# Position bias added by VectorE from a 128-fold stored table, and second-block attention groups first

## What is computed

```python
# layer 0: 12 heads, banded, with a bias by distance; q and k are normed per head
bias = rel_bias[:, jnp.clip(rel, -REL_CLIP, REL_CLIP) + REL_CLIP]
s = einsum('bqhd,bkhd->bhqk', qc, kc) * scale + bias
s = jnp.where(valid, s, NEG_INF);  p = softmax(s);  o = p @ v
# layer 1: 6 pairs of heads, chunk mask, difference of two softmaxes, norm of each output
a = p[:, :, 0] - lam * p[:, :, 1];  o = rmsnorm(a @ v, b_subln) * (1.0 - lambda_init)
# both layers: 4 more heads attend to a memory, with no bias
# layer 2: 8 heads of 128, causal, with a T5 bias by distance
```

## Time and profile before

| | us |
|---|---|
| median of 3 runs | 2204.18 |
| lowest, highest | 2199.34, 2204.64 |
| the profiled execution's own time | 2210.05 |
| its span, first to last instruction | 2208.3 |

### The profile page before, as it was taken

How to read it: one execution, slowest core, us unless ns; L and a number is a source line. 1 busy time by engine, 2 the same in 40 slices (tenths; PEclk the granted TensorE clock), 3 DMA queues, 4 the chain that set the end, 5 groups by cost and what they waited for, 6 DMA issues and landing times.

```text
span 2208.3 us, 27753 instructions
## 1 busy us (share of the span) xinstructions
PE 2040.2 (92%) x11973; PEld 1392.1 (63%) x11973; DVE 837.6 (38%) x973; ACT 693.9 (31%) x917; POOL 35.1 (2%) x27
## 2 busy tenths in 40 slices
PE   7999999999999997899999999989888888989886
PEld 6998777899899876799977644433333333333332
DVE  5555644555555577555543521111111111111112
ACT  5444564544644455443434211111101000110010
POOL 6000000000000000000000000000000000000000
PEclk9999999999999998999999899999999999999998
DMA  8554606555455541355463699999999999999995
GB/s 278 193 191 152 210 11 209 160 190 184 150 193 190 171 153 58 115 191 183 141 210 115 267 403 428 427 428 428 427 428 428 427 428 428 427 428 427 427 428 215
DMA packets 164820, 604.21 MB, mean 274 GB/s; under 512 B 9204, under 2 KB 102336, under 8 KB 140052
## 3 DMA queue, kind: packets, MB, share of 16 engines
q1 hardware_dynamic: 164724, 602.82, 70.9%
HBM read 601.70 MB, written 1.09 MB: 273 GB/s over the span
## 4 chain that ended last, share of the span: by engine, by line
PE 61%; DMA 28%; ACT 5%; DVE 4%; issue 1%; SPq 1%; DVEq 0%; ACTq 0%
PE ps L1432 14%; PE ps L1434 14%; PE ps L1433 14%; DMA sb_raw<-in_moe_w_gate_up 10%; PE ps L1791 8%; DMA sb_w_free<-in_moe_w_gate_up 8%; DMA sb_nat_more<-in_moe_w_gate_up 6%; PE ps L1801 4%; DMA sb_raw<-in_moe_w_down 3%; PE ps L1606 1%; ACT sb_w_hi L589 1%; ACT sb_prob L704 1%; PE ps L1808 1%; PE ps L1774 1%; PE ps L1566 1%
## 5 line engine op out<-in xcount | busy, mean ns | idle before, releaser
L893 DVE TENSOR_TENSOR sb_w_lo<-sb_raw,sb_w_hi 128x2048 fp32r<-128x2048 f32 x180 | 415.7, 2312 | 369.3 <-ACT sb_w_hi L589 369.0
L589 ACT ACTIVATE sb_w_hi<-sb_raw 128x2048 fp32r<-128x2048 f32 x180 | 343.9, 1914 | 295.0 <-PE ps L1434 283.3
L1432 PE MATMUL ps<-sb_xT_hi,sb_w_hi 128*128 128x256 f32 x1408 | 397.3, 282 | 7.2 <-DVE sb_xT_lo L914 7.2
L1433 PE MATMUL ps<-sb_xT_lo,sb_w_hi 128*128 128x256 f32 x1408 | 396.2, 281 | 0.0
L1434 PE MATMUL ps<-sb_xT_hi,sb_w_lo 128*128 128x256 f32 x1408 | 396.1, 281 | 0.0
L1432 PEld LDWEIGHTS ps<-sb_xT_hi,sb_w_hi 128*128 128x128 f32 x1408 | 265.9, 189 | 9.8 <-issue 4.5
L1433 PEld LDWEIGHTS ps<-sb_xT_lo,sb_w_hi 128*128 128x128 f32 x1408 | 266.0, 189 | 1.6
L1434 PEld LDWEIGHTS ps<-sb_xT_hi,sb_w_lo 128*128 128x128 f32 x1408 | 266.0, 189 | 0.0
L1791 PE MATMUL ps<-sb_raw,sb_xs 128*64 128x512 f32 x784 | 177.5, 595 | 23.7 <-DMA sb_raw<-in_moe_w_gate_up 23.3
L1791 PE MATMUL ps<-sb_w_free,sb_xs 128*64 128x512 f32 x752 | 172.1, 602 | 27.0 <-DMA sb_w_free<-in_moe_w_gate_up 26.4
L1432 PE MATMUL ps<-sb_w_hi,sb_xT_hi 128*128 128x512 f32 x384 | 155.1, 404 | 9.2 <-DVE sb_xT_lo L914 4.7
(11 more groups left out here) (245 smaller groups left out, 2334.2 us busy)
## 6 DMA issues: line engine op xcount, KB each, us to landing
sb_raw<-in_moe_w_gate_up SPq DMA_DIRECT2D x49, 2048.0 KB, 35.4
sb_w_free<-in_moe_w_gate_up SPq DMA_DIRECT2D x47, 2048.0 KB, 35.3
sb_w_free<-in_moe_w_down SPq DMA_DIRECT2D x25, 2048.0 KB, 35.4
sb_raw<-in_moe_w_down SPq DMA_DIRECT2D x23, 2048.0 KB, 34.0
sb_raw<-in_ffn_w_gate SPq DMA_DIRECT2D x44, 1024.0 KB, 5.4
sb_raw<-in_ffn_w_up SPq DMA_DIRECT2D x44, 1024.0 KB, 5.3
sb_raw<-in_ffn_w_down SPq DMA_DIRECT2D x44, 1024.0 KB, 4.9
sb_late_raw<-in_moe_w_gate_up SPq DMA_DIRECT2D x16, 2048.0 KB, 35.4
```

Source lines behind the costliest of these rows:

```text
L589: sc.activation(w_hi[:, c % CUT, :], raw[:, c % RAW, :], ACT.Copy).then_inc(hi_made, 1)
L893: ve.tensor_tensor(w_lo[:, c % CUT, :], raw[:, c % RAW, :], w_hi[:, c % CUT, :].bitcast(F32), ALU.subtract).then_inc(lo_made, 1)
L1432: pe.matmul(o, l_hi, r_hi, start=start, stop=False)
L1433: pe.matmul(o, l_hi, r_lo, start=False, stop=False)
```

## The change

- `ext` in DRAM becomes 24 blocks of 128 rows of 512. `store_rows` writes each head's row 128 times (a source that repeats, 256 KB a head). `load_strips` reads at a pitch of 511, from element 127 on, so that partition p gets the window that begins at 127 - p: the strips are no longer reversed.
- The `flip` products of layers 0 and 2 are gone. `lead` adds strip and scores on VectorE (PSUM and SBUF in, `prob` in SBUF out), then takes the maximum from `prob`; `exps` reads `prob` in these groups. The waits for the strips go from TensorE to VectorE. Layer 1's mask stays a product.
- In all three attentions the groups of own heads of block 1 (256 keys) now come before those of block 0. Memory groups keep their order. Block 1's rows are turned first. In layer 1 the turn of block 1 comes after outputs(7), `sub_norm(1)` after outputs(6), `sub_norm(0)` after outputs(7), and both square roots after ScalarE's last copy.

```diff
+EXT_ROW = P * 512
-        ext = nc.dram_tensor("ext", (3, 12, 512), F32)
+        ext = nc.dram_tensor("ext", (2 * 12, EXT_ROW), F32)
-            order = [(b, h0) for b in range(TB) for h0 in (0, 4, 8)]
+            order = [(b, h0) for b in (1, 0) for h0 in (0, 4, 8)]
             if kind == "rel":
-                order = [(b, h0) for b in range(TB) for h0 in (0, 4)] + [(b, 8) for b in range(TB)]
+                order = [(b, h0) for b in (1, 0) for h0 in (0, 4)] + [(b, 8) for b in (1, 0)]
             if kind == "moba":
-                for b in range(TB):
+                for b in (1, 0):
...
                 sp.wait_ge(ext_copied, n + 1)
-                sp.dma_start(ext[n, 0:heads, :], row_by_distance(heads)).then_inc(ext_stored, 16)
+                dst = bass.AP(ext, n * 12 * EXT_ROW, [[EXT_ROW, heads], [512, P], [1, 512]])
+                src = row_by_distance(heads).unsqueeze(1).to_broadcast([heads, P, 512])
+                sp.dma_start(dst, src).then_inc(ext_stored, 16)
                 sp.wait_ge(ext_stored, 16 * (n + 1))
...
-                    src = bass.AP(ext, (n * 12 + h0 + h) * 512, [[1, P], [1, REL_W]])
+                    src = bass.AP(ext, (n * 12 + h0 + h) * EXT_ROW + P - 1, [[511, P], [1, REL_W]])
...
                     for h in range(4):
-                        src = ps[:, 2 * p + h % 2, (h // 2) * S:(h // 2) * S + g["nk"] * P]
+                        if g["bias"] and not g["diff"]:
+                            src = prob[:, p, h, 0:g["nk"] * P]
+                        else:
+                            src = ps[:, 2 * p + h % 2, (h // 2) * S:(h // 2) * S + g["nk"] * P]
...
+                        for c in range(2):
+                            ve.tensor_tensor(prob[:, p, 2 * c:2 * c + 2, 0:nk], s[:, c, :, 0:nk], rows,
+                                             ALU.add).then_inc(biased, 1)
+                        for c in range(2):
+                            ve.wait_ge(biased, biased_no[0] - 1 + c)
+                            ins = ve.tensor_reduce(soft[:, p, 2 * c:2 * c + 2], prob[:, p, 2 * c:2 * c + 2, 0:nk], AX.X,
+                                                   ALU.max, negate=True)
...
-                        if groups[n]["diff"] and n >= 5 and n != 6:
-                            sub_norm(int(n == 7))
+                        if groups[n]["diff"] and n >= 6:
+                            sub_norm(7 - n)
...
                         for h in pair:
-                            if g["bias"]:
-                                h0, _ = g["bias"]
+                            if g["diff"]:
                                 m0 = P if g["b"] == 0 else 0
-                                if kind == "diff":
-                                    ins = pe.matmul(at(h), flip_bf[:], chunk_mask[:, m0:m0 + nk], start=False, stop=True)
-                                else:
-                                    row = strip[:, h0 + h, m0:m0 + nk] if h0 < 8 else strip_b[:, h, m0:m0 + nk]
-                                    ins = pe.matmul(at(h), flip[:], row, start=False, stop=True)
+                                ins = pe.matmul(at(h), flip_bf[:], chunk_mask[:, m0:m0 + nk], start=False, stop=True)
...
                         if n == len(groups) - 1:
                             pe.wait_ge(prob_made, u0 + len(groups))
-                            first_block()
+                            if not g_last_diff:
+                                first_block()
                         outputs(n)
                         if n == 0:
                             scores(2)
+                    if g_last_diff:
+                        first_block()
```

More of the change, by code:

```diff
@@ L797, in _ @@
                     sub_root(1)
+                    sub_root(0)
                 turn(t_of(i, T_O))
@@ L1062, in lead @@
                         ve.wait_ge(probT_turned, u - 1)
-                    for c in range(2):
-                        ins = ve.tensor_reduce(soft[:, p, 2 * c:2 * c + 2], s[:, c, :, 0:g["nk"] * P], AX.X, ALU.max, negate=True)
+                    nk = g["nk"] * P
+                    if g["bias"] and not g["diff"]:
+                        if u0 == u_moba:
+                            ve.wait_ge(strip_loaded, 16 * 20)
+                        else:
+                            ve.wait_ge(strip_ready, g["bias"][0] // 8 + 1)
+                        m0 = P if g["b"] == 0 else 0
+                        for c in range(2):
+                            h0 = g["bias"][0] + 2 * c
+                            rows = strip[:, h0:h0 + 2, m0:m0 + nk] if h0 < 8 else strip_b[:, h0 - 8:h0 - 6, m0:m0 + nk]
+                            ve.tensor_tensor(prob[:, p, 2 * c:2 * c + 2, 0:nk], s[:, c, :, 0:nk], rows,
+                                             ALU.add).then_inc(biased, 1)
+                            biased_no[0] += 1
+                        for c in range(2):
+                            ve.wait_ge(biased, biased_no[0] - 1 + c)
+                            ins = ve.tensor_reduce(soft[:, p, 2 * c:2 * c + 2], prob[:, p, 2 * c:2 * c + 2, 0:nk], AX.X,
+                                                   ALU.max, negate=True)
+                    else:
+                        for c in range(2):
+                            ins = ve.tensor_reduce(soft[:, p, 2 * c:2 * c + 2], s[:, c, :, 0:nk], AX.X, ALU.max,
+                                                   negate=True)
                     ins.then_inc(max_made, 1)
@@ L1442, in keep_busy, with turn @@
                         pe.matmul(ps[:, bank, 0:P], ident[:], ident[:], start=True, stop=True)
-            def turn(src, ready, count, blocks=range(TB)):
-                for b in blocks:
-                    pe.wait_ge(ready, count + b)
+            def turn(src, ready, count, blocks=range(TB), last=TB - 1):
+                for m, b in enumerate(blocks):
+                    pe.wait_ge(ready, count + m)
                     for q in range(4):
@@ L1550, in scores @@
                         pe.wait_ge(prob_made, u - 1)
-                    if kind == "moba":
-                        pe.wait_ge(strip_loaded, 16 * 20)
-                    elif n >= 2:
+                    if n >= 2 and kind != "moba":
                         pe.wait_ge(tiles_copied, 16 * (w + 1))
-                        if kind == "rel":
-                            pe.wait_ge(strip_ready, g["bias"][0] // 8 + 1)
-                        else:
-                            pe.wait_ge(mask_made, 3)
+                    if g["diff"]:
+                        pe.wait_ge(mask_made, 3)
                     q0 = g["b"] * P
@@ L1612, in attend @@
                 last = g_in(w) + 5 if w < 2 else g_moba + 6
+                g_last_diff = groups[-1]["diff"]
                 def opening():
@@ L1693, in _ @@
                 project(g_in(i), c_in(i), 5, t_of(i, T_MIX), between)
-                remainder(later_tiles, lambda: turn(nat, *rows_made, range(1)))
+                remainder(later_tiles, lambda: turn(nat, *rows_made, (1,), last=0))
                 pe.wait_ge(o_made, u_layer(i) + 8)
-                turn(nat, *rows_made, range(1, TB))
+                turn(nat, rows_made[0], rows_made[1] + 1, (0,), last=0)
                 project(g_out(i), c_out(i), 2, t_of(i, T_O))
@@ L1721, in _ @@
             project(g_moba, c_moba, 6, t_moba, between)
-            remainder(None, lambda: turn(nat, o_made, u_moba + 2, range(1)))
-            turn(nat, o_made, u_moba + 3, range(1, TB))
+            remainder(None, lambda: turn(nat, o_made, u_moba + 2, (1,), last=0))
+            turn(nat, o_made, u_moba + 4, (0,), last=0)
             project(g_moba_out, c_moba_out, 2, t_moba_o)
```

22 lines of the change are left out of this document (11 added, 11 removed).

## The result

| | median, us | runs | ratio to before, 95% |
|---|---|---|---|
| before (same chips) | 2204.4 (2199.3 to 2206.7) | 4 | |
| after | 2274.2 (2269.3 to 2278.2) | 4 | 1.032 [1.029, 1.035] |

The change makes the kernel 70 us slower, where I had forecast 52 us. The profiled execution of after took 2274.3 us (span 2272.5 us, mean granted clock 0.963; before 2210.05, 2208.3 and 0.979). It lies on its own median, while the one of before was 5.6 us above its own; so the two profiles differ by 64.2 us and the medians by 70.

The account below looks back on a forecast made before the run. It took TensorE (61% of the span's chain) and DMA (28%) as bounds. Stalls 32.7 + 30.3, plus 4 for clock, less 14.6 gained, gave +52.4 us: 2256.6 us on the median, predicted as 2257; 8-in-10 range 2238 to 2274.

Parts of the forecast that it names:

- the store: Bias rows stored in layers 0 and 2, at 81 and 54 GB/s: 38.6 us for either, 39 us more than now.
- the gains: Savings in the three attentions: 3 us in layer 0, 7 in layer 1, 4.6 in layer 2, together 14.6 us.
- Rival B: Both stores slower still, at the small stores' burst rates, 49.5 and 44 us more: +68 us, 2272 us; chance 0.12.
- rival A: Both stores run at their engines' rate, 9.8 us each: -10.9 us, 2193 us, not slower; chance 0.10.
- The stalls: TensorE waits for chunk 4 of the projection: 32 us in layer 0 (32.7 with the norms), 30.3 us in layer 2.
- Tail 0: Layer 0's attention, values(0) to projection out: 45.5 us becomes 40.0; 3 us gained after clock losses (0 to 5.5).
- The loop: VectorE and ScalarE turn in layer 0's attention becomes the bound: 4.9 us for 256 keys, 3.4 us for 128.
- the half clock: Idle TensorE falls to clock 0.50 in layer 0's last outputs, values and turns, taking 1 to 5 us back.
- rival C: Adds bound VectorE, TensorE at half clock in all tails; layers 0, 2, 1 gain nothing, two, five: +60 us, 2264; within forecast's 0.78.
- Tail 1: End of layer 1's attention: new group order starts the projection out at 881.9 instead of 889.0; 7 us gained (5 to 8).
- Tail 2: Layer 2's attention: projection out starts at 1211.7 instead of 1216.3; 4.6 us gained, 2 if the clock falls.
- The base: Whole kernel: the sum was put on the median of the runs, 5.9 us below the profiled 2210.05 us.

Follow-up runs that it names:

- best: The changed kernel with rows stored once and spread by a copy inside DRAM, and chunk 4's weights issued ahead of that store; 2198.3 us, ratio 0.9968.
- after2: The changed kernel once more, unaltered, for a second profile; that profiled execution took 2276.4 us.
- again: The kernel before, unchanged, for a second profile; that profiled execution took 2204.45 us.
- adds: As best, but with the old order of the groups, so the adds alone without stalls; 2211.3 us, ratio 1.0028.
- holes: As best, with 12 and 11 idle TensorE products ahead of the outputs of groups 1 and 5 in layer 0's attention; 2199.1 us, ratio 0.9956.
- order: The kernel before with only the new order of groups, keeping flip products and small store; 2198.9 us, ratio 0.9975, and 2199.3 us, 0.9965, when repeated.

## Why the prediction came out as it did

I predicted 2256.6 us and a range up to 2274; it is 2274.2, 0.2 us beyond the range. The direction, the cause and its two places were right. What failed are the sizes of two parts of the sum, the store and the gains. Whole kernels show it without any marks: from `best`, which has all of the change but its stalls, to after it is 76 us (2198.3 to 2274.2), where I had 67.0 for stalls and clock; from before to `best` 6.5 us are gained (2204.8 to 2198.3), where I had 14.6. Rival B's 2272 us is nearer than mine, but by luck: its store is too slow in layer 0 (49.5 us more, measured 43.1), and its gains are the same 14.6. The 17.6 us missing are, term by term (profile of after against the first of before):

**The store, sized too short: 8.1 us.** I took 38.6 us for the data and 39 for the excess; the excess was 43.1 and 43.0. Scaling 217 GB/s down to 12 and 8 partitions gave 81 and 54 GB/s; the stores made 76 and 51 alone, 74 and 50 beside the rest of the kernel. The data time is 42.7 us (235.8 to 278.5), and 1.9 us lie around it, from issue to first packet and from the last to SP's next issue. They nearly cancel in the excess, since the small store held SP for 1.5 us with hardly any data. So the miss is the rate: 42.7 us of data where the 32-partition row, scaled down, gave 38.6. The measured 43 lie between my 39 and rival B's 49.5 and 44; the 9.8 us of rival A are refuted.

**The stalls** follow from the store by the cover, as written. Layer 0: 43.1 - 7.0 = 36.1, less 3.0 because chunk 4 landed in 5.4 us and not in 8.4: 33.1, and TensorE was empty for 33.2. From there to V0 after lost another 3.3 us, where I had 0.7 for the norms and 2 for the clock. Another 2.2 us of the +38.7 lie ahead of the store (it was issued at 234.25 instead of 232.05), in a part that the change doesn't touch. Layer 2: 43.0 - 8.7 = 34.3; TensorE was empty for 37.0, since in after it had done its first group 2.7 us sooner, at full clock. Net +36.0, where I had 32.3.

**Tail 0, the wrong sign: 6.7 us.** I had 3 us gained, and it was 3.7 lost in this execution; in `after2` it was 0.7 lost against `again`, and 0.8 gained against the first of before. The loop was sized right, within 0.15 us a turn. The step that failed is the price of the half clock, "1 to 5 us back" out of a gain of 5.5 for the adds: the adds alone gain nothing (`adds` is 0.3 and 1.8 us longer than before). I had priced the fall to half clock at one place, the end, where the kernel before has it too; the adds make two holes in TensorE's work, at 8 and 28 us behind V0, and a stretch at half clock follows each. `holes` gets 2.7 us back by filling them and ends at 42.1 us; my hand schedule had 40.0, and the 2 us between are not traced. Two things hid the size of this miss. The new order, for which I had put down nothing in layer 0, gains 2.1 to 3.5 us there (`order`); and the 45.3 us that I started from were 1.4 us longer than in `again`. So rival C, with nothing gained in layer 0, was right there, but not in layer 2, where it has 2 us gained and 4.8 were. One small thing I had at zero: four exponentials of 256 keys that read SBUF start 0.49 us apart, and 0.45 from PSUM (2.0 us for four in `best`, 1.8 in before).

**Tail 1, within its range: 6.1 for 7** (5.1 against `again`; I had 5 to 8). Here is the chain of waits at its end in after:

```profile
912.77 0.34 DVE sb_soft L1105 x2
...
916.22 1.66 DVE sb_nat_more L1163 x6
...
919.84 1.67 DVE sb_nat_more L1163 x6
...
923.81 0.76 PE ps L1459
```

From the first line, in the last follow, to the projection it is 11.0 us, where I had counted 11.5 and before had 12.5 from the same instruction; no table load stands ahead of it any more. `order` has the same tail without the adds, so the gain is the order's.

**Tail 2, right: 4.8 for 4.6.** That the opening costs TensorE nothing holds only with the adds: eight large scores take 3.6 us in `best`, and with their flips 7.1 in `order`. So this gain does belong to both parts together.

**The base: 5.9 us.** I subtracted from the sum what lay between the profiled execution and the median of before. The profile of after had no such excess (0.1 us), so the subtraction was one-sided. This is no step of the mechanism: the 5.6 us by which `again` is shorter are spread over five stages, 0.9 to 1.4 us in each, tails 0 and 1 among them. 8.1 + 6.7 + 5.9 are 20.7; the small terms (landing -3.0, earlier start of the store +2.2, tails +0.7, clock and norms +0.3, and -3.3 in all stages that the change doesn't touch) bring it to the 17.6.

**Not settled.** Why the clock of one and the same stage differs between executions; in layer 2 that is worth 0 to 4 us (94.5 to 98.2 us with the same code), as much as what separates the best variants. Open too are the 2 us of tail 0 between `holes` and my hand schedule, and whether filled holes make the whole kernel faster. A store from more partitions (the rows made on every fourth one) wasn't tried in the kernel.

## What to carry to other kernels

Ask of a DMA not only how many bytes and engines it has but out of which partitions it comes: here four neighbours shared one way out of some 25.6 GB/s, and rows that were stored once and spread inside DRAM held the queue for 13.7 us instead of 44.6. Look next at what stands behind a wait in the queue that also issues the weights, and count its cover in microseconds. Work taken off the bounding engine only pays if that engine doesn't fall idle by it: here the adds lost 3.0 us of layer 0's tail to the flip products, 2.7 of them by half clock. Dummy products in two idle stretches brought these back in the tail of one profile, but not in the time of the kernel, so measure both. When parts of a change are bundled, run them apart: here the slow store cost 76 us (after against `best`), the adds 6 alone and nothing beside the new order, and the order gained 6 to 8.

## What the runs showed of the hardware

- Stores out of SBUF, GB/s: 51 from 8 neighbouring partitions, 76 from 12, 102 from 16, 210 from 32, 387 from 128; but 205 from 8 partitions four apart. Repeating the source row (a step of 0) saves nothing: 24 KB read 128 times over took 42.7 us, as 3.15 MB at 76 GB/s.
- Twelve partitions four apart were slower than eight, 150 against 205 GB/s.
- From DRAM to DRAM 3.15 MB went at 301 GB/s with 12 rows outermost and at 315 with 128, into the same order that the store from SBUF wrote at 76.
- The DMA share shown is of engines held, not of rate: 0.92 at 102 GB/s, 1.03 at 387.
- In `best` TensorE stood idle for 3.56 us and then ran 306 to 312 us at clock 0.50. With 12 idle products of 512 columns in that gap (`holes`) the same stretch ran at 1.00, and a shorter one behind it, 312 to 316 us, at 0.65.
